# Attention: five of VectorE's low-half subtractions of weight units are issued behind the next pair of maps' masked sums and copy instead of ahead of them

## What is computed

```python
proj = h @ w_in[l]
(qa, ka, va, qb, kb, vb, qc, kc, vc, fc, gc, qlat, kvlat, kidx, widx) = jnp.split(proj, split_points, axis=-1)
o_a = _diff_attention(...)        # two softmaxes a head: p[:, 0] - lam * p[:, 1]
o_b = _moba_attention(...)        # bias by distance, own block only at this length
o_c = _forgetting_attention(...)  # logits + cumulative forget gates
o_d = _dsa_attention(...)         # softmax over the 64 keys that the indexer scores highest
x = x + g1 * (jnp.concatenate([o_a, o_b, o_c, o_d], axis=-1) @ w_out[l])
```

## Time and profile before

| | us |
|---|---|
| median of 3 runs | 723.14 (723.1 to 723.15) |
| the profiled execution, its own time | 724.23 |
| its span, first to last instruction | 722.4 |
| TensorE matmul busy | 698.9 (97% of the span) |
| VectorE busy | 501.1 (69%) |
| ScalarE busy | 397.3 (55%) |
| low-half subtractions on VectorE (line 1650), 97 of them | 237.0 |
| mean granted TensorE clock | 0.991 of full speed |

### The profile page before, as it was taken

The page is one execution under the profiler, slowest core; times in us unless marked ns, Lnnn a source line. Parts: engine busy times, 40 slices in busy tenths (PEclk is TensorE's granted clock), DMA queues, the critical chain, the costliest instruction groups (busy, mean ns, idle before and its releaser), DMA issues.

```text
span 722.4 us, 15359 instructions
## 1 busy us (share of the span) xinstructions
PE 698.9 (97%) x6436; PEld 659.9 (91%) x6436; DVE 501.1 (69%) x901; ACT 397.3 (55%) x639; POOL 122.4 (17%) x96
## 2 busy tenths in 40 slices
PE   7899999999999999999999999989999999999995
PEld 6798988899999999999999998869999999999993
DVE  1454888647888879797666478863687666666666
ACT  2258646834746465656446674663574555544552
POOL 2001003004054635453010000300400000000002
PEclk9999999999999999999999999999999999999998
DMA  9999987465485857588753874646526577555511
GB/s 329 392 275 287 391 282 280 176 233 176 131 316 196 292 176 293 175 291 284 279 162 116 303 271 150 229 180 235 175 88 210 137 244 248 184 175 175 182 52 58
DMA packets 97739, 159.43 MB, mean 221 GB/s; under 512 B 6119, under 2 KB 84744, under 8 KB 91400
## 3 DMA queue, kind: packets, MB, share of 16 engines
q1 hardware_dynamic: 97672, 158.46, 64.0%
HBM read 156.81 MB, written 1.64 MB: 219 GB/s over the span
## 4 chain that ended last, share of the span: by engine, by line
PE 78%; DVE 9%; ACT 5%; issue 3%; SPq 2%; DMA 1%; POOL 0%; DVEq 0%; POOLq 0%; ACTq 0%
PE bank L965 23%; PE bank L966 22%; PE bank L967 22%; PE bank L978 3%; DVE w_lo L1650 2%; ACT work L1535 2%; DVE score L1831 1%; DMA own_bias<-in_buckets 1%; PE bank L1258 1%; ACT w_hi L1396 1%; DVE top L1830 1%; PE bank L1011 1%; SPq L711 1%; SPq L731 1%; PE bank L1289 1%
## 5 line engine op out<-in xcount | busy, mean ns | idle before, releaser
L1650 DVE TENSOR_TENSOR w_lo<-raw,w_hi 128x2048 fp32r<-128x2048 f32 (+1 forms) x97 | 237.0, 2443 | 96.6 <-ACT w_hi L1396 96.4
L965 PE MATMUL bank<-act_hi,w_hi 128*128 128x256 f32 (+1 forms) x1024 | 292.9, 286 | 0.8 <-DVE act_lo L1667 0.7
L966 PE MATMUL bank<-act_lo,w_hi 128*128 128x256 f32 (+1 forms) x1024 | 289.6, 283 | 0.0
L967 PE MATMUL bank<-act_hi,w_lo 128*128 128x256 f32 (+1 forms) x1024 | 289.6, 283 | 0.0
L1396 ACT ACTIVATE w_hi<-raw 128x2048 fp32r<-128x2048 f32 (+1 forms) x97 | 183.0, 1888 | 143.8 <-PE bank L967 133.3
L965 PEld LDWEIGHTS bank<-act_hi,w_hi 128*128 128x128 f32 (+1 forms) x1024 | 195.5, 191 | 4.5 <-issue 3.4
L966 PEld LDWEIGHTS bank<-act_lo,w_hi 128*128 128x128 f32 (+1 forms) x1024 | 195.6, 191 | 0.4
L967 PEld LDWEIGHTS bank<-act_hi,w_lo 128*128 128x128 f32 (+1 forms) x1024 | 195.5, 191 | 0.0
L1952 DVE SCALAR_TENSOR_TENSOR work<-bank,vec,work 128x254 f32<-128x254 f32 (+1 forms) x176 | 76.5, 476 | 11.1 <-ACT work L1594 9.6
L965 PE MATMUL bank<-mlp_hi,w_hi 128*128 128x256 f32 x192 | 54.7, 285 | 0.0
L966 PE MATMUL bank<-mlp_lo,w_hi 128*128 128x256 f32 x192 | 54.3, 283 | 0.0
(11 more groups left out here) (205 smaller groups left out, 942.8 us busy)
## 6 DMA issues: line engine op xcount, KB each, us to landing
direct<-in_w_ada SPq DMA_DIRECT2D x48, 1024.0 KB, 8.6
raw<-in_w_ffn_up SPq DMA_DIRECT2D x44, 1024.0 KB, 5.2
raw<-in_w_ffn_down SPq DMA_DIRECT2D x22, 1024.0 KB, 4.9
raw<-in_w_in SPq DMA_DIRECT2D x21, 1024.0 KB, 6.5
raw<-in_w_out SPq DMA_DIRECT2D x8, 1024.0 KB, 5.0
bias<-toeplitz SPq DMA_DIRECT2D x4, 384.0 KB, 11.6
xT<-in_x SPq DMA_DIRECT2D x1, 1024.0 KB, 5.1
raw<-in_w_in SPq DMA_DIRECT2D x2, 512.0 KB, 11.0
```

The source lines that it names most:

```text
L965: pe.matmul(dst, lh, rh, start=first, stop=False, skip_group_check=check)
L966: pe.matmul(dst, lh, rl, start=False, stop=False, skip_group_check=check)
L967: return pe.matmul(dst, ll, rh, start=False, stop=last, skip_group_check=check)
L1650: nc.vector.tensor_tensor(w_lo[n % RAW][:, s], raw[n % RAW][:, s], w_hi[n % RAW][:, s].bitcast(F32), ALU.subtract).then_inc(lo_done, 1)
```

## The change

Five `split_lo` entries of the list are put later, in both layers. The subtractions of units 7, 8, 12 and 13 now stand behind the pair of maps that followed them. That of unit 9 stands behind one round of the choice and the pair of maps. Every other entry stays.

```diff
@@ -257,15 +257,16 @@
         split(6)
     second_half(4)
     s += [("index", 0), ("index", 1), ("forget_up", 0), ("index", 2), ("index", 3)]
-    split(7)
+    s.append(("split_hi", 7))
     first_half(5)
     maps()
+    s.append(("split_lo", 7))
     second_half(5)
     s.append(("split_hi", 8))
     mix()
-    s.append(("split_lo", 8))
     first_half(6)
     maps()
+    s.append(("split_lo", 8))
     pair()
     choice()
     mix()
@@ -275,10 +276,10 @@
     s.append(("split_hi", 9))
     maps()
     mix()
-    s.append(("split_lo", 9))
     choice()
     first_half(7)
     maps()
+    s.append(("split_lo", 9))
     pair()
     mix()
     choice()
@@ -310,11 +311,11 @@
     s.append(("split_hi", NI))
     maps()
     mix()
-    s.append(("split_lo", NI))
     first_half(10)
     if l == 0:
         pair()
     maps()
+    s.append(("split_lo", NI))
     mix()
     second_half(10)
     if l == 0:
@@ -322,9 +323,9 @@
     s.append(("split_hi", NI + 1))
     maps()
     mix()
-    s.append(("split_lo", NI + 1))
     first_half(11)
     maps()
+    s.append(("split_lo", NI + 1))
     s.append(("turn", 0))
     mix()
     second_half(11)
```

## The result

| | changed | before, same chip |
|---|---|---|
| median of the runs | 719.43 us (719.13 to 720.68, 4 runs) | 723.14 us (723.1 to 723.6, 4 runs) |
| ratio | 0.9925, 95% interval 0.99 to 0.995 | |
| the profiled execution, its own time | 720.68 us | 724.23 us |
| its span | 718.8 us | 722.4 us |
| mean granted TensorE clock | 0.992 | 0.991 |

The change made the kernel faster. The medians differ by 3.7 us (0.5%). The measured ratio puts the gain at 0.75%: 723.14 times it is 717.7 us, a gain of 5.4 us, with an interval from 715.9 to 719.5 us (3.6 to 7.2 us of gain). So the size of the gain is known to about 2 us from this measurement.

What follows compares the result with a forecast made beforehand. TensorE was taken to bound most of the attention, VectorE's stream a few points. Layer 0 0.0, layer 1 -2.75 and clock -1.6 make -4.35 us, from 723.14 to 718.8 us; range 717.8 to 722.0.

Steps and rivals of the forecast that it cites:

- Layer 0: -1.0 + 1.26 - 0.2 = 0.0: Layer 0's attention: gains at units 8, 9 and 13 offset by unit 12's new wait, net 0.0 us.
- Units 8 and 9, -1.0 in layer 0: Early maps: TensorE's waits at 91.06 and 97.92 shrink by 0.40 and 0.6 us, making it 1.0 us earlier.
- Unit 12 in layer 0, +1.26: Ahead of map 16's scores: the later subtraction delays the scaling and ScalarE's copy of unit 10; TensorE waits 1.26 us.
- Unit 13, -0.2 in layer 0 and nothing in layer 1: At the heads' transposes: 0.2 us gained in layer 0; nothing in layer 1, where its place already waits for scores.
- Unit 12 in layer 1, -2.75 in all: Map 16's scores come 2.75 us earlier, including 1.0 us from units 8 and 9; a wait of about 1.6 us stays.
- Unit 7, nothing: Sums of maps 0 and 1 come earlier, but no TensorE wait hangs on them: no gain.
- The clock, -1.6: Behind layer 1's scores of map 16: the fall to 1.2 GHz likely goes, saving 1.6 us; the least sure term.
- The loads, nothing: SP queue loads wait for later low halves, up to 4 us for unit 12 in layer 0; costed at nothing.
- Contention, nothing: GpSimd work beside moved subtractions: none expected; beside unit 12's in layer 1 it would cost up to 0.87 us.
- the clock term fails: Rival, chance 0.28: the clock fall stays in layer 1 or unprofiled runs never had it; 720.4 us.
- a new fall in layer 0: Rival, chance 0.11: layer 0's new 1.26 us wait lowers the clock there and the old fall stays; 722.0 us.
- Slower: Rival, chance 0.07: unit 12's subtraction costs in both layers, with a clock fall in layer 0; 725.0 us.

Runs made afterwards that it cites:

- unit 8 alone: The kernel before with only unit 8's subtraction moved later; 722.33 us against 723.84, ratio 0.9982.
- unit 9 alone: The kernel before with only unit 9's subtraction moved later, in both layers; 721.66 us, ratio 0.9973.
- unit 12 alone: The kernel before with only unit 12's subtraction moved later, in both layers; 723.5 us, ratio 0.9997.
- the filled kernel of before: The kernel before with four unread identity matmuls in layer 1's wait ahead of map 16's scores; 723.03 us against 723.93, ratio 0.9993.
- units 7 and 13 back: The changed kernel with the subtractions of units 7 and 13 put back in their old places; 720.11 us, ratio 0.9941.
- unit 12 moved in layer 1 only: The changed kernel with unit 12's subtraction back ahead of the sums in layer 0, still moved in layer 1; 718.41 us, ratio 0.9918.

## Why the prediction failed in size, and what of it was right

The forecast was a fall of 4.35 us, to 718.8. The profiles give 4.9 us for the attention, the medians 3.7 and, measured again, 5.0, and the ratio of the first measurement 5.4 us, which is 717.7 us, just below the range. Every mechanism of the likeliest case was seen. The step that failed is the size of the term "Layer 0: -1.0 + 1.26 - 0.2 = 0.0": layer 0 gained 0.44 us. The term was also added wrongly, since its parts make +0.06. Each part missed by 0.04 to 0.3 us in the same direction. In layer 1 the total was right (4.45 us, forecast 4.35) while two parts were not: the clock is worth 1.3 us there and not 1.6, and unit 13 gives 0.25 us and not nothing. That these two cancel is luck, and so is a median as near to 718.8 as 719.43: the first chip's medians show 1.2 us less than the profiles.

- **Units 8 and 9, -1.0 in layer 0.** Map 8 comes 0.99 us earlier from map 0 (27.00 to 26.01), the forecast 1.0. Unit 8's part is 0.36 by its own experiment (forecast 0.40), unit 9's 0.61 (forecast 0.6). But layer 0 as a whole gained 0.44, and with the new wait at 1.1 and unit 13 at 0.24 the front must have given 1.3. The further 0.3 us appears between maps 8 and 10, in layer 0 alone: in "unit 8 alone" too the scores of map 10 are 0.65 us ahead, 0.29 more than those of map 8, and with unit 9 alone they are not. It lies inside the products of map 8's scores. In the trace of before they and the transposes behind them read 97.92 and

```profile
99.16 0.55 PE L1258 MATMUL bank<-ident,work 128*128 128x128 f32 x3
```

1.24 us apart, the first three products taking 0.76 us; with unit 8 alone moved it is 0.95 us and 0.47:

```profile
97.34 0.47 PE L1147 MATMUL bank<-qkT 64*128 64x128 f32 x3 [0.57 <-ACT qkT L1476]
...
98.29 0.55 PE L1258 MATMUL bank<-ident,work 128*128 128x128 f32 x3
```

  No row names a wait for it, so I had counted these 0.29 us as work; what holds TensorE there isn't settled. It doesn't need unit 8's move: in the disturbed profile of "unit 12 alone" the way from map 8 to map 10 is 9.86 us as well, against 10.16 before.
- **Unit 12 in layer 0, +1.26.** The wait shown is 1.07 us and its removal gave 1.11. The order of events was as forecast: the sums when the scores are there, the subtraction last ahead of the scaling, then ScalarE's copy of unit 10, then the scores of map 16. I had the subtraction begin when the last read of the sums has ended; the rows above show it beginning with that read, at 128.56. The scaling thus comes 1.16 us later than with unit 12 behind it (58.54 against 57.38 from map 0), not 1.26.
- **Unit 13, -0.2 in layer 0 and nothing in layer 1.** 0.24 us, and 0.25 us in layer 1. The nothing was wrong: the idle time of 0.51 us at 485.20 in the earlier trace rows was read behind a stretch at the lower clock, where TensorE is late and VectorE waits for it. With the clock at full speed layer 1 looks as layer 0 does: its heads' transposes wait 0.64 us in "unit 8 alone" and "unit 9 alone", where the clock doesn't fall, and 0.40 us in the profile of before.
- **Unit 12 in layer 1, -2.75 in all.** Map 16 comes at 56.90 instead of 59.76 us from map 0: 2.86 us. The sums of map 14 started at 469.71 in the profile, or 468.87 on the clock of before (less the 0.84 us by which this layer's map 0 was late); the forecast was 468.9. The new wait ahead of map 16 is 1.56 us, forecast about 1.6.
- **Unit 7, nothing.** Shown by putting it back: the waits and the times at maps 0 to 16 didn't change.
- **The clock, -1.6.** Layer 1 gained 4.45 us, of which 2.86 stood at map 16; the remaining 1.6 us is 1.33 of the clock and 0.25 of unit 13. The 1.33 comes from the filled kernel of before, and it fits three more profiles without the fall: layer 1's gain of 1.68 us with unit 8 alone, 2.78 with unit 9 alone and 2.36 with unit 12 alone is 0.35, 1.46 and 1.03 at map 16, and 1.3 behind it each time. As a statement on the median the term was too simple. With the same two waits the fall in layer 1 stands in some profiles and not in others, and how often the changed kernel escapes it isn't shown; its two profiles have none. The rival "the clock term fails" was half right in this sense: filling the wait in the kernel before moved the median by 0.9 us with an interval that includes nothing.
- **The loads, nothing.** The largest group of the unit products waited 0.4 us in the whole program, most of it for `act_lo` and not for a low half of a unit:

```profile
L966 PE MATMUL bank<-act_hi,w_hi 128*128 128x256 f32 (+1 forms) x1024 | 293.2, 286 | 0.4 <-DVE act_lo L1668 0.3
```

- **Contention, nothing.** Unit 12's subtraction took 2.29 us in both layers. The forecast priced any GpSimd work beside it at up to 0.87 us, and its row was misread: the instruction beside the subtraction at 111.37 is the gain's multiplication, not the squares. In the trace of before 20 of the 128x2048 subtractions overlap with GpSimd work. The 13 that began while a GpSimd instruction was running took 2.58 to 5.50 us; the 7 that began first took 2.28 or 2.29, as one without company does. One of each kind:

```profile
111.09 1.29 POOL L909 TENSOR_TENSOR heads_out<-heads_out,gain 128x512 f32<-128x512 f32 x1
...
161.63 2.29 DVE L1650 TENSOR_TENSOR w_lo<-raw,w_hi 128x2048 fp32r<-128x2048 f32 x1 [1.04 <-ACT w_hi L1396]
...
162.28 2.23 POOL L888 TENSOR_TENSOR work<-work 128x256 f32<-128x256 f32 x1 [33.65 <-ACT work L1405]
```

  So what counts is whether GpSimd is already at work when the subtraction starts, and the price can exceed 0.87 us by far: the longest, 5.50 us, is 3.2 us more than 2.29.

The rival "a new fall in layer 0" didn't come: behind the new wait of 1.07 us the clock is 1.00 in both profiles of the changed kernel. This stretch of the changed kernel had TensorE busy for 2.93 of 4.00 us:

```profile
130.00:134.00 4.00, 2.93 (x27) 2.10 (x26) 2.98 (x11) 3.03 (x4) 0.00 (x0) 1.00 0.51 160
```

"Slower" was decided where I had put it: the sums of map 14 in layer 1 came 2.8 us ahead of the point from which it decides. What no step of the prediction had is the start. The two profiles of the changed kernel differ there by 0.8 us (map 0 at 72.22 and 71.44), and all thirteen, which have the same TensorE work up to there, lie between 69.51 and 72.72, so spans may not be compared without counting from the same instruction.

What the change gave up is now plain too. Taking a subtraction from ahead of the sums paid at units 8, 9 and 13, in layer 1 at unit 12, and did nothing at unit 7. But unit 12's was put between the sums and the scaling, where TensorE hangs on the scaling through ScalarE's copy. One entry later the kernel is another 1.7 us faster.

## What to carry to other kernels

When long filler work moves behind a short step, ask what the engine waits for next: the filler is free only up to the length of that wait (1.41 us at unit 9's place took in 1.4 of its 2.2 us), and beyond it, it delays whatever hangs on the step after, through other engines' queues as well. Try the place one entry further before accepting the new wait. And cut profiles that differ in their start at a common instruction: here 4.9 us of gain showed as 3.6 in the span.

## What the runs showed of the hardware

The granted clock of one kernel differs between executions. At the start the stretch at 1.2 GHz was 7 us long in one profile of the changed kernel and 3.4 us in the other. In the kernels that differ from it only later it was 3.5 us (before), none at all ("units 7 and 13 back", 1.00 from 8 to 34 us), and in "unit 12 moved in layer 1 only" it was 10 us, with TensorE busy throughout:

```profile
9.50:19.50 10.00, 10.00 (x106) 8.79 (x105) 1.87 (x7) 0.68 (x1) 1.23 (x2) 0.50 1.07 377
```

This execution took 720.05 us, and the kernel's median is 718.41, so a single profile with such a fall says little of the kernel. In layer 1 stretches with TensorE busy for 1.02, 0.93, 0.94 and 0.88 of 3.40 us were followed by a granted clock of 0.50, 0.60, 1.00 and 1.00. The Trainium skill, page "TensorE: Matmul & The Clock Gate", (section "Part 1: The HAM clock gate"), says of the start that the number of slow matmuls varies from run to run of one kernel; the two profiles of the changed kernel agree (7 and 3.4 us of slow clock). Inside the kernel, some 475 us in, these stretches show a like variation, between kernels that differ by one or two moved subtractions. For a change that lives on the clock this means that its gain is a share of the executions, to be read from many runs, and never from one trace.
